# Where the opening of a fused kernel's second part puts its elementwise work

## The chip, the cores and the metric

The program runs on one core of a Trainium2 chip. Its time is the device time in microseconds (us) of one launch, which computes the whole output. The figure for a kernel is the median of its runs.

## What is computed

Two networks run one after the other on 512 tokens of width 1024, in float32. The first has two layers of differential attention beside a gated recurrence, each with an MLP and a gated embedding. Its last step is a norm, `rms_norm(h, g_final)`, and the result is the input of the second network. That is a state-space mixer (8 groups of heads, 6 chunks of 128 tokens, two directions) over 256 context tokens and the 512 tokens, then an attention mixer. Each mixer's input is normed, scaled and shifted:

```python
x = rms_norm(h, g_final)                                   # end of the first network
in_lat = rmsnorm(h_lat, norm_w[i]) * (1.0 + scl) + sh      # h_lat = x for i = 0
in_ctx = rmsnorm(h_ctx, norm_w[i]) * (1.0 + sclc) + shc
z, xbc, dt = split(in @ in_w)                              # state-space mixer
xbc = silu(conv5(xbc) + b); dt = softplus(dt + bias)       # steps: 64 columns
la = cumsum(dt * a) per chunk; to_end = exp(la_end - la) * dt
h_lat = h_lat + gt * out(...)
```

So at the seam there are two norms in a row, and x itself is kept as the residual of the first mixer.

## The kernel before

Activations lie with features on the 128 partitions (8 blocks, `KB`) and tokens along the free dimension. A float32 product is made of three products of rounded parts: each operand is split into a rounded `hi` and the rest `lo` (`value - hi`). Weights stream from memory as 1 MB tiles in two slots. SyncE issues the loads. GpSimd splits each tile when TensorE has released its slot: four roundings (L404), then four rests (L408), in one long loop over pairs of tiles (`split_pair`). TensorE's `dense` (its products are L797) goes through the 8 feature blocks of a tile and can wait before each block.

Every engine runs its own instruction list in order and waits on semaphores. These lists are written out by hand, so the order of the work around the change is the order in the source.

*The seam.* TensorE sums squares over the features and gives two rows, broadcast over the partitions: PSUM bank 6 holds the reciprocal root of the first norm, bank 7 the factor of the second norm on top of the first. VectorE then works on a feature block b of 512 tokens with three instructions: `scaled` (L2296) multiplies the residual `hres` by g_final and bank 6, in place; `normed_in` (L2303) multiplies it by bank 7 into `tin`; `rest_in` (L2307) writes `inlo`. Between the last two ScalarE scales and shifts `tin` (L1590) and rounds it to `inhi` (L1591). `tin` has two buffers, so `normed_in(b)` waits for `rest_in(b-2)`. VectorE also makes both rests of the context (L2292). ScalarE then issues the DMA that spills `hres` to memory (L1592); it is read back, and its place reused, in the groups.

*The steps.* TensorE's first product is that of the step tile, fed block by block (`in_lo`). VectorE adds the bias (L2333), TensorE turns it token-major (L818), VectorE copies it (L2336), ScalarE takes Abs and Exp (L1624, L1626), VectorE runs the softplus (L2885 to L2893), and L2339, L2340 add the positive part. Meanwhile TensorE computes four blocks of 128 channels (`T_XS0`, `T_BC0`), and later their cumulative sums (L831, L833).

*The first filters.* For each of the four blocks ScalarE copies it from PSUM and makes the first tap (`first_copy`, L1611 to L1613, L1598), VectorE adds four taps (`first_conv`, L2363), ScalarE takes a tanh (`conv_tanh`, L1617, L1618) and VectorE gates (`silu`, L2377). Between blocks 1 and 2 VectorE reads the cumulative sums (L2396 to L2400), and ScalarE makes exponentials of them (L1641 to L1644). After block 3 VectorE makes two tables (L2408, L2409) and clears five tiles (L2410 to L2415). The last of the clears but one releases ScalarE into the first group.

*The first group.* ScalarE: a tanh (L1659), a copy (L1664), copies of the turned chunks (L1668, L1669). TensorE turns chunks (L862 to L864), four before it needs ScalarE's first copies.

*The half-norms.* After the groups the residual is normed again in two halves of 384 tokens (`half_in`): VectorE's product (L2445), ScalarE's scale and shift by segment of tokens (L1761) and rounding (L1765), VectorE's rest (L2439). The first half has two segments, since context and tokens have different factors, the second one.

*Small parts.* `second_params` (L1935 to L1952) prepares scale and shift vectors during the first network's last stage. `busy` (L479) gives TensorE small products while it waits.

## Time and profile before

| | us |
|---|---|
| runs shown | 2400.40, 2401.42, 2402.52 (median 2401.42) |
| the profiled execution: its time | 2399.92 |
| its span, first to last instruction | 2397.9 |
| mean granted clock of TensorE | 0.990 |
| busy: TensorE, VectorE | 2310.2 (96%), 1497.4 (62%) |
| busy: ScalarE, GpSimd | 755.2 (31%), 1418.5 (59%) |
| chain that ended last | TensorE 75%, VectorE 16%, "issue" 3%, ScalarE 3%, DMA 1%, GpSimd 1% |

In the profile PE is TensorE, PEld its weight loads, DVE VectorE, ACT ScalarE, POOL GpSimd. Times run from the span's first instruction. A line such as L797 is a line of the kernel's source. "Idle before <-" names what ended the idle time of the engine ahead of an instruction. An instruction's length takes in any time in which it stands started but held up. The chain is followed back from the last instruction, at each step to what released it. Clock 1.00 stands for 2.4 GHz, 0.5 for 1.2 GHz. The second part begins near 1266 us, its groups at 1336 us, its attention near 2048 us.

### The profile page before, as it was taken

The page shows a single profiled execution, that of the slowest core. Times are in us where ns is not written, and L with a number is a line of the kernel's source. Part 1 is how long each engine was busy: PE and PEld are TensorE (multiplying, and loading weights), DVE is VectorE, ACT ScalarE, POOL GpSimd, SP SyncE. Part 2 cuts the span into 40 slices and gives each one's busy share as a digit, 9 for nine tenths or more (in the row PEclk, how much of TensorE's full clock was granted, in tenths as well). Part 3 has the DMA queues.
Part 4 walks back from the last instruction along what each step waited for, and adds up shares of the span by engine and source line. Part 5 has one row for each costly group of instructions (what it writes and reads, how often), then busy time and mean ns, then how long its engine had stood idle before and what let it go on. Part 6 is the DMA issues. An engine that isn't in the chain of part 4 may idle for free.

```text
span 2397.9 us, 32255 instructions
## 1 busy us (share of the span) xinstructions
PE 2310.2 (96%) x11638; PEld 1905.7 (79%) x11638; DVE 1497.4 (62%) x1868; ACT 755.2 (31%) x1579; POOL 1418.5 (59%) x1248
## 2 busy tenths in 40 slices
PE   8999999999999899999998999999999998999998
PEld 6767888888777688888877899999999987776446
DVE  7964333444784552434478888788788787518653
ACT  2453200112333430110135434334334334533551
POOL 8735767777776277777784353453453451256785
PEclk9999999999999999999999999999999998999999
DMA  4321334433224033434332110111110112021212
GB/s 166 112 74 71 132 140 141 158 132 121 90 74 129 30 129 121 152 134 155 106 116 102 53 53 35 52 52 35 52 52 35 52 53 82 29 95 58 52 28 71
DMA packets 41596, 211.31 MB, mean 88 GB/s; under 512 B 5408, under 2 KB 9504, under 8 KB 21536
## 3 DMA queue, kind: packets, MB, share of 16 engines
q1 hardware_dynamic: 27456, 164.84, 19.4%
q10 hardware_dynamic: 14048, 45.17, 5.6%
q8 instruction: 67, 1.10, 0.2%
q14 instruction: 25, 0.20, 0.0%
HBM read 197.67 MB, written 7.34 MB: 85 GB/s over the span
## 4 chain that ended last, share of the span: by engine, by line
PE 75%; DVE 16%; issue 3%; ACT 3%; DMA 1%; POOL 1%; ACTq 0%; DVEq 0%; SPq 0%; POOLq 0%
PE ps L505 39%; PE ps L797 15%; PE ps L1044 5%; DVE convd L2363 2%; PE ps L1161 2%; PE ps L894 1%; PE ps L1143 1%; DVE wdec L2507 1%; PE ps L917 1%; PE ps L599 1%; PE ps L641 1%; PE ps L1148 1%; DVE convd L2377 1%; PE ps L622 1%; DVE convd L2359 1%
## 5 line engine op out<-in xcount | busy, mean ns | idle before, releaser
L404 POOL TENSOR_SCALAR whi<-wraw 128x512 fp32r<-128x512 f32 x564 | 385.4, 712 | 909.5 <-PE ps L797 423.0
L408 POOL TENSOR_TENSOR wlo<-wraw,whi 128x512 fp32r<-128x512 f32 x568 | 859.4, 1544 | 0.8 <-ACT whi L1401 0.8
L505 PE MATMUL ps<-uhi,whi 128*128 128x512 f32 x896 | 353.4, 394 | 15.5 <-POOL wlo L390 11.0
L505 PE MATMUL ps<-uhi,wlo 128*128 128x512 f32 x896 | 349.5, 390 | 0.0
L505 PE MATMUL ps<-ulo,whi 128*128 128x512 f32 x896 | 349.5, 390 | 0.0
L797 PE MATMUL ps<-inhi,whi 128*128 128x384 f32 (+1 forms) x784 | 243.1, 345 | 5.5 <-DVE inlo L2307 4.3
L797 PE MATMUL ps<-inhi,wlo 128*128 128x384 f32 (+1 forms) x784 | 235.9, 335 | 0.0
L797 PE MATMUL ps<-inlo,whi 128*128 128x384 f32 (+1 forms) x784 | 235.8, 335 | 0.0
L505 PEld LDWEIGHTS ps<-uhi,whi 128*128 128x128 f32 x896 | 168.7, 188 | 54.3 <-POOL wlo L390 11.0
L2182 DVE TENSOR_TENSOR h<-h,ps 128x1024 f32<-128x1024 f32 x40 | 48.8, 1221 | 241.4 <-PE ps L505 241.4
L505 PE MATMUL ps<-hidhi,whi 128*128 128x512 f32 x512 | 199.2, 389 | 0.0
L505 PE MATMUL ps<-hidhi,wlo 128*128 128x512 f32 x512 | 199.2, 389 | 0.0
L505 PE MATMUL ps<-hidlo,whi 128*128 128x512 f32 x512 | 199.2, 389 | 0.0
L505 PEld LDWEIGHTS ps<-uhi,wlo 128*128 128x128 f32 x896 | 168.8, 188 | 36.3 <-issue 1.4
L505 PEld LDWEIGHTS ps<-ulo,whi 128*128 128x128 f32 x896 | 168.7, 188 | 35.4
L1492 ACT ACTIVATE hsq<-hm 128x1024 f32<-128x1024 f32 x32 | 34.0, 1064 | 488.2 <-DVE hm L2213 488.2
L797 PEld LDWEIGHTS ps<-inhi,whi 128*128 128x128 f32 (+1 forms) x784 | 143.7, 187 | 16.8 <-issue 8.6
L2363 DVE SCALAR_TENSOR_TENSOR convd<-raw,cpg,convd 128x770 f32<-128x770 f32 x128 | 149.0, 1164 | 5.0 <-ACT convd L1598 2.6
L2213 DVE SCALAR_TENSOR_TENSOR hm<-ps,rstd 128x1024 f32<-128x1024 f32 x32 | 39.2, 1225 | 173.3 <-PE ps L505 173.2
L797 PEld LDWEIGHTS ps<-inhi,wlo 128*128 128x128 f32 (+1 forms) x784 | 144.5, 187 | 1.0
L797 PEld LDWEIGHTS ps<-inlo,whi 128*128 128x128 f32 (+1 forms) x784 | 144.4, 187 | 0.8
L1690 ACT ACTIVATE ebuf<-ps,tabg 128x128 f32<-128x128 f32 x384 | 104.4, 387 | 116.8 <-PE ps L906 83.8
(450 smaller groups left out, 4628.1 us busy)
## 6 DMA issues: line engine op xcount, KB each, us to landing
wraw<-in_wstream SPq DMA_DIRECT2D x150, 1024.0 KB, 4.8
modraw<-in_modw ACTq DMA_DIRECT2D x48, 512.0 KB, 3.3
hspill<-hres ACTq DMA_DIRECT2D x1, 3072.0 KB, 10.6
...
```

Source lines behind the costliest of these rows:

```text
L404: pool.tensor_scalar(whi[:, s, c], wraw[:, s, c], 1.0, 0.0, ALU.mult, ALU.add).then_inc(wraw_read, 1)
L408: ins = pool.tensor_tensor(wlo[:, s, c], wraw[:, s, c], whi[:, s, c].bitcast(F32), ALU.subtract)
L505: mm = pe.matmul(ps[:, 2 * bank + m, :], a[:, w, c:c + P], b[:, kb, :], start=(n == 0 and i == 0), stop=(n == KB - 1 and i == 2))
L599: pe.matmul(ps[:, SCORE_BANKS(n)[c], 0:w], q, proj[64 * c:64 * c + 64, K0 + hd, 0:w], start=True, stop=False)
L797: mm = pe.matmul(ps[0:width, q + half, 0:HALF], a[:, s, c:c + width], b[:, kb, half * HALF:(half + 1) * HALF], start=(n == 0), stop=(n == ...
L1044: mm = pe.matmul(ps[:, q + m, :], a[:, k % 2, c:c + P], b[:, kb, t0:t0 + S], start=(kb == 0 and i == 0), stop=(kb == KB - 1 and i == 2))
L1161: mm = pe.matmul(ps[64 * e:64 * e + 64, 2, :], vtok2[:, kb, HD * j:HD * j + HD], pT2[(NC * b + kb) % RING][:, e, :], start=(kb == 0), stop ...
L1492: A(hsq[n % 2][:, :, :], hm[n % 2][:, :, :], ACT.Square).then_inc(L["sqh_r"], 1)
L1690: ins = A(ebuf[:, d, r, :], ps[:, 4 + d, r * P:(r + 1) * P], ACT.Exp, bias=tabg[:, K_NB + 2 * c + d, r:r + 1])
L2182: V.tensor_tensor(h[:, 2 * j:2 * j + 2, :], h[:, 2 * j:2 * j + 2, :], TWO(bank), ALU.add).then_inc(L["h_r"], 1)
L2213: V.scalar_tensor_tensor(out=hm[n % 2][:, :, :], in0=TWO(n % 2), scalar=0.0, in1=rstd2, op0=ALU.max, op1=ALU.mult).then_inc(L["m_r"], 1)
L2363: ins = V.scalar_tensor_tensor(out=o, in0=r[:, n:n + CW], scalar=cpg[:, 6 * b + n:6 * b + n + 1], in1=o, op0=ALU.mult, op1=ALU.add)
```

## The change

- The factor of `normed_in` now holds g_final, the second norm's weight and 1 + scale at once (`modA` is multiplied by g_final), and bank 7 holds the reciprocal root of both norms together. VectorE's `scaled` is gone. The shift is added by ScalarE in its rounding pass and by VectorE in its rest, both as one instruction a block. The same is done in the half-norms, where product and rest now go by segment.
- The residual is scaled by GpSimd, in place, two instructions a block, each block after VectorE's product has read it; ScalarE copies bank 6 into `row6` for that. GpSimd also makes the second half of the context rest. Its long loop is cut in three, and these instructions stand between the split of tile 103 and that of tile 104.
- ScalarE reads the step product, TensorE turns it inside the next tile (ahead of its third block), Abs reads PSUM. The spill is issued behind GpSimd's last block and ahead of Abs.
- VectorE no longer copies the cumulative sums: ScalarE copies one into the table and takes its exponentials from PSUM. The order of filters and gates changes on VectorE and ScalarE, and the two tables come ahead of the last filter.
- Three clears go to a place ahead of the norm terms on VectorE, two to GpSimd behind the split of tile 106. The first group waits for the tables and not for a clear. Counts of semaphores that stand later are adapted.

```diff
--- before.py
+++ after.py
@@ gpsimd @@
+        def first_zeros():
+            pool.wait_ge(dt_d, DT_END)
+            pool.memset(lablk[:, :, :].bitcast(F32), 0.0)
+            pool.wait_ge(spill, 16)
+            pool.memset(sqz[:, :, :], 0.0).then_inc(sqz_r, 1)
...
-        with pool.Fori(NFM // 2 + 1, (T_ATT + 11) // 2) as i:
+        with pool.Fori(NFM // 2 + 1, T_XS0 // 2 + 1) as i:
+            split_pair(i)
+        pool.wait_ge(ctx_hi, 2)
+        pool.tensor_tensor(inlo[:, 4:8, 0:CTX], ctxn[:, 4:8, :], inhi[:, 4:8, 0:CTX].bitcast(F32), ALU.subtract
+                           ).then_inc(ctx_t, 1)
+        pool.wait_ge(rr_r, 1)
+        for b in range(KB):
+            pool.wait_ge(in_t, b + 1)
+            pool.tensor_scalar(hres[:, b, CTX:T], hres[:, b, CTX:T], p2[:, C2_GF + b:C2_GF + b + 1], None, ALU.mult
+                               ).then_inc(n_x, 1)
+            pool.wait_ge(n_x, 2 * b + 1)
+            pool.tensor_tensor(hres[:, b, CTX:T], hres[:, b, CTX:T], row6[:, :], ALU.mult).then_inc(n_x, 1)
+        split_pair(T_G0 // 2)
+        split_pair(T_G0 // 2 + 1, between=first_zeros)
+        with pool.Fori(T_G0 // 2 + 2, (T_ATT + 11) // 2) as i:
@@ tensor @@
         def turn_dt():
-            pe.wait_ge(dt_d, 1)
+            pe.wait_ge(dt_a, 2)
...
-        turn_dt()
         wait_split(T_XS0)
-        dense(T_XS0 % 2, lambda i: i * TM, P, IN, EIGHT, False, 2, None)
+        dense(T_XS0 % 2, lambda i: i * TM, P, IN, EIGHT, False, 2, None, lambda kb: turn_dt() if kb == 2 else None)
@@ scalar @@
+        act.wait_ge(rb_ps, 2)
+        A(row6[:, :], ps[:, 6, :], ACT.Copy).then_inc(rr_r, 1)
         for b in range(KB):
             act.wait_ge(in_t, b + 1)
-            st(A(tin[:, b % 2, 0:S], tin[:, b % 2, 0:S], ACT.Identity, scale=modA[:, b, 0:1], bias=modv[0][:, b, 0:1]))
-            A(inhi[:, b, CTX:T], tin[:, b % 2, 0:S], ACT.Copy).then_inc(in_hi, 1)
-        act.dma_start(hspill, hres[:, :, :]).then_inc(spill, 16)
+            A(inhi[:, b, CTX:T], tin[:, b % 2, 0:S], ACT.Identity, bias=modv[0][:, b, 0:1]).then_inc(in_hi, 1)
...
-        act.wait_ge(dt_d, 2)
-        A(dtw[1][:, :, :], dtw[0][:, :, :], ACT.Abs).then_inc(dt_a, 1)
-        act.wait_ge(dt_a, 2)
+        done_wait(T_DT)
+        A(halves(dtT[:, :]), ps[0:64, 0:2, 0:HALF], ACT.Identity, bias=p2[0:64, C2_DTB:C2_DTB + 1]).then_inc(dt_a, 1)
+        act.wait_ge(n_x, 2 * KB)
+        act.dma_start(hspill, hres[:, :, :]).then_inc(spill, 16)
+        act.wait_ge(dt_p, 1)
+        A(dtw[1][:, :, :].rearrange("p c r -> p (c r)"), ps[:, 4, 0:384], ACT.Abs).then_inc(dt_a, 1)
+        act.wait_ge(dt_a, 3)
...
         first_copy(0, 1, None)
+        conv_tanh(0, 0)
         first_copy(1, None, T_XS0)
-        conv_tanh(0, 0)
         conv_tanh(0, 1)
         first_copy(2, 2, None)
-        act.wait_ge(dt_d, DT_C)
+        act.wait_ge(dt_p, 2)
+        A(flat(K_G), ps[:, 5, 0:384], ACT.Copy).then_inc(dt_a, 1)
+        act.wait_ge(dt_d, DT_C)
         A(w(6), w(6), ACT.Ln).then_inc(dt_a, 1)
-        A(flat(K_EXLA), w(3), ACT.Exp)
-        A(flat(K_DEC), w(4), ACT.Exp)
+        A(flat(K_EXLA), ps[:, 5, 0:384], ACT.Exp)
+        A(flat(K_DEC), ps[:, 6, 0:384], ACT.Exp)
...
-        act.wait_ge(acc_r2, 1)
+        act.wait_ge(dt_d, DT_END)
...
(half_in, for each segment)
-                    ins = A(tin[:, b % 2, t0:t1], tin[:, b % 2, t0:t1], ACT.Identity, scale=modA[:, b, c:c + 1],
-                            bias=modv[1][:, b, c:c + 1])
-                st(ins)
-                A(inhi[:, b, hs], tin[:, b % 2, hs], ACT.Copy).then_inc(in_hi, 1)
+                    ins = A(inhi[:, b, t0:t1], tin[:, b % 2, t0:t1], ACT.Identity, bias=modv[1][:, b, c:c + 1])
+                ins.then_inc(in_hi, 1)
@@ vector @@
+            st(V.tensor_tensor(modA[:, :, 0], modA[:, :, 0], gf, ALU.mult))
...
+        V.memset(larow[:, :, :].bitcast(F32), 0.0)
+        V.tensor_copy(lapick[:, :], picks[:, :])
+        V.memset(acc[:, :], 0.0).then_inc(acc_r2, 1)
         dve.wait_ge(L["mod_T"], DEPTH * PER["mod_T"] + 1)
...
-        st(V.reciprocal(dcol[:, 16:24], dcol[:, 8:16]))
-        V.tensor_tensor(dcol[:, 20:24], dcol[:, 20:24], dcol[:, 8:12], ALU.mult).then_inc(n_rs, 1)
+        V.reciprocal(dcol[:, 16:24], dcol[:, 8:16]).then_inc(n_rs, 1)
...
(scaled(b) is removed; normed_in and rest_in of block b:)
-            V.tensor_tensor(tin[:, b % 2, 0:S], hres[:, b, CTX:T], ps[:, 7, :], ALU.mult).then_inc(in_t, 1)
+            V.scalar_tensor_tensor(out=tin[:, b % 2, 0:S], in0=hres[:, b, CTX:T], scalar=modA[:, b, 0:1], in1=ps[:, 7, :],
+                                   op0=ALU.mult, op1=ALU.mult).then_inc(in_t, 1)
...
-            V.tensor_tensor(inlo[:, b, CTX:T], tin[:, b % 2, 0:S], inhi[:, b, CTX:T].bitcast(F32), ALU.subtract
+            V.scalar_tensor_tensor(out=inlo[:, b, CTX:T], in0=tin[:, b % 2, 0:S], scalar=modv[0][:, b, 0:1],
+                                   in1=inhi[:, b, CTX:T].bitcast(F32), op0=ALU.add, op1=ALU.subtract).then_inc(in_lo, 1)
...
         first_conv(0)
+        silu(0, 0)
         first_conv(1)
-        silu(0, 0)
         silu(0, 1)
-        dt(V.tensor_copy(w(3), ps[:, 5, 0:384]))
-        dt(V.tensor_copy(tab[:, K_G:K_G + 2 * NC, :].rearrange("p c r -> p (c r)"), ps[:, 5, 0:384]))
-        dt(V.tensor_copy(w(4), ps[:, 6, 0:384]))
-        dt(V.tensor_tensor(w(5), w(4), w(3), ALU.subtract))
         dt(V.tensor_scalar(w(6), w(2), 1e-37, None, ALU.max))
+        dve.wait_ge(dt_a, 5)
+        dt(V.tensor_tensor(w(5), ps[:, 6, 0:384], flat(K_G), ALU.subtract))
         first_conv(2)
+        dve.wait_ge(dt_a, 7)
+        dt(V.tensor_tensor(flat(K_NB), w(6), flat(K_G), ALU.subtract))
+        dt(V.tensor_tensor(flat(K_TE), w(5), w(2), ALU.mult))
         first_conv(3)
         silu(0, 2)
         silu(0, 3)
...
```

## Rows read from the trace of the kernel before

**Rows 1.** Busy time of each engine by window, 1272 to 1287 us: length, busy us (instructions), clock, DMA

```profile
1272.00:1287.00 15.00, 11.15 (x48) 6.73 (x48) 12.89 (x26) 11.08 (x16) 0.00 (x0) 0.89 0.13 52
```

**Rows 2.** Timeline of VectorE: start, length, line, operation, output<-inputs, idle before

```profile
1265.74 0.16 DVE L2282 TENSOR_SCALAR dcol<-ps 128x4 f32<-128x4 f32 x1 [3.65 <-PE ps L735]
...
1276.50 0.68 DVE L2307 TENSOR_TENSOR inlo<-tin,inhi 128x512 fp32r<-128x512 f32 x1
1277.11 0.74 DVE L2296 SCALAR_TENSOR_TENSOR hres<-hres,p,ps 128x512 f32<-128x512 f32 x1
...
1278.36 0.68 DVE L2307 TENSOR_TENSOR inlo<-tin,inhi 128x512 fp32r<-128x512 f32 x1
...
1285.10 0.69 DVE L2307 TENSOR_TENSOR inlo<-tin,inhi 128x512 fp32r<-128x512 f32 x1 [0.70 <-ACT inhi L1591]
```

**Rows 3.** Timeline of GpSimd near the kernel's start

```profile
26.12 0.62 POOL L388 TENSOR_SCALAR whi<-wraw 128x512 fp32r<-128x512 f32 x1
26.82 1.28 POOL L390 TENSOR_TENSOR wlo<-wraw,whi 128x512 fp32r<-128x512 f32 x1
```

**Rows 4.** Instructions of one line: ns min/median/max, first and last start

```profile
L408 POOL TENSOR_TENSOR wlo<-wraw,whi x3: 1261/1700/1715, 1259.8 to 1263.2; 128x512 fp32r<-128x512 f32 x3
...
L408 POOL TENSOR_TENSOR wlo<-wraw,whi x4: 1983/2007/2011, 1310.5 to 1316.4; 128x512 fp32r<-128x512 f32 x4
...
L2377 DVE SCALAR_TENSOR_TENSOR convd<-raw,convd x32: 949/962/2046, 1313.2 to 1966.2; 128x770 f32<-128x770 f32 x32
```

**Rows 5.** Timeline of VectorE in the first half-norm

```profile
2050.77 1.65 DVE L2439 TENSOR_TENSOR inlo<-tin,inhi 128x384 fp32r<-128x384 f32 x1 [1.14 <-ACT inhi L1765]
2052.46 0.56 DVE L2445 TENSOR_TENSOR tin<-oacc,ps 128x384 f32<-128x384 f32 x1
```

**Rows 6.** Timeline of all engines at the hand-over to softplus

```profile
1287.15 1.01 DVE L2333 TENSOR_SCALAR dtT<-ps,p 64x768 f32<-64x768 f32 x1 [1.30 <-PE ps L797]
...
1288.22 0.59 PE L818 MATMUL ps<-ident,dtT 64*128 64x64 f32 x6 [1.10 <-DVE dtT L2333]
...
1290.70 0.45 DVE L2885 TENSOR_SCALAR dtw<-dtw 128x384 f32<-128x384 f32 x1 [1.22 <-ACT dtw L1626]
```

**Rows 7.** Timeline of VectorE through the first filters

```profile
1307.74 5.56 DVE L2363 SCALAR_TENSOR_TENSOR convd<-raw,cpg,convd 128x770 f32<-128x770 f32 x4 [0.96 <-ACT convd L1598]
...
1317.16 0.55 DVE L2396 COPY dtw<-ps 128x384 f32<-128x384 f32 x1
...
1319.52 0.36 DVE L2400 TENSOR_SCALAR dtw<-dtw 128x384 f32<-128x384 f32 x1
...
1325.69 7.35 DVE L2363 SCALAR_TENSOR_TENSOR convd<-raw,cpg,convd 128x770 f32<-128x770 f32 x4 [1.59 <-ACT convd L1598]
```

**Rows 8.** Timeline of ScalarE through the first filters

```profile
1313.67 0.61 ACT L1618 ACTIVATE raw<-convd 128x512 f32<-128x512 f32 x1
1315.36 0.39 ACT L1611 ACTIVATE raw<-ps 128x256 f32<-128x256 f32 x1 [1.09 <-DVE convd L2377]
...
1316.34 1.03 ACT L1598 ACTIVATE convd<-raw,cpg 128x770 f32<-128x770 f32 x1
```

**Rows 9.** Timelines of TensorE and of ScalarE at the first group's start

```profile
1336.21 0.41 PE L862 MATMUL ps<-ident,convd 128*128 128x128 f32 x2 [2.90 <-DVE convd L2377]
...
1341.03 0.45 PE L862 MATMUL ps<-ident,convd 128*128 128x128 f32 x2 [0.77 <-ACT btok L1669]
...
1338.79 0.81 ACT L1659 ACTIVATE zs<-ps 128x768 f32<-128x768 f32 x1 [4.78 <-DVE acc L2413]
```

**Rows 10.** Timeline of ScalarE in the first and the second half-norm

```profile
2057.74 0.99 ACT L1761 ACTIVATE tin<-tin,modv,modA 128x256 f32<-128x256 f32 x2
2058.76 0.52 ACT L1765 ACTIVATE inhi<-tin 128x384 fp32r<-128x384 f32 x1
...
2077.77 0.71 ACT L1761 ACTIVATE tin<-tin,modv,modA 128x384 f32<-128x384 f32 x1
```

**Rows 11.** Chain of waits in order of time: start, us, engine, line

```profile
1233.04 0.19 DVE modA L1936
```

More of the change, by code:

```diff
@@ L181, in build @@
     ctxr = at("ctxr", 138, [P, CTX])
+    row6 = at("row6", 186.375, [P, S])
     dcol = at("dcol", 142, [P, 32])
@@ L394, in _, with split_pair @@
             pool.sem_inc(wfree, 1)
-        def split_pair(i, rounded=None):
+        def first_zeros():
[3 more added lines that the diff above has]
+            pool.memset(sqz[:, :, :], 0.0).then_inc(sqz_r, 1)
+        def split_pair(i, rounded=None, between=None):
             for s in range(2):
+                if s and between:
+                    between()
                 pool.wait_ge(wland[s], i * 16 + 16)
@@ L767, in half_sums @@
                 busy(2, 7)
-            pe.wait_ge(rr_r, 2 + h)
+            pe.wait_ge(rr_r, 3 + h)
             for c in range(3):
@@ L812, in _, with input_wait @@
         busy(11, 0)
-        dense(T_DT % 2, lambda i: i * 64, 64, IN, EIGHT, True, 0, None, lambda kb: pe.wait_ge(in_lo, kb + 1))
+        def input_wait(kb):
+            pe.wait_ge(in_lo, kb + 1)
+            if kb == 4:
+                pe.wait_ge(ctx_t, 2)
+        dense(T_DT % 2, lambda i: i * 64, 64, IN, EIGHT, True, 0, None, input_wait)
         def turn_dt():
-            pe.wait_ge(dt_d, 1)
+            pe.wait_ge(dt_a, 2)
             for c in range(NC):
@@ L984, in _ @@
         group(GROUPS - 1, True)
-        pe.wait_ge(rr_r, 1)
+        pe.wait_ge(rr_r, 2)
         half_sums(0)
@@ L1671, in group @@
             act.wait_ge(lr_ps, g + 1)
+            act.wait_ge(sqz_r, g + 1)
             for r in range(HPG):
@@ L1744, in half_squares @@
                 n = KB * hf + j
-                act.wait_ge(n_x, KB + n + 1)
+                act.wait_ge(n_x, 2 * KB + n + 1)
                 if n >= 6:
@@ L2331, in _ @@
         dt = Chain(dve, dt_d)
-        done_wait(T_DT)
-        dt(V.tensor_scalar(halves(dtT[:, :]), ps[0:64, 0:2, 0:HALF], p2[0:64, C2_DTB:C2_DTB + 1], None, ALU.add))
         w = lambda n: dtw[n][:, :, :].rearrange("p c r -> p (c r)")
-        dve.wait_ge(dt_p, 1)
-        dt(V.tensor_copy(w(0), ps[:, 4, 0:384]))
-        dve.wait_ge(dt_a, 3)
+        dve.wait_ge(dt_a, 4)
         softplus(V, dt, w(2), w(1), w(3), w(4), w(5))
-        dt(V.tensor_scalar(w(0), w(0), 0.0, None, ALU.max))
-        dt(V.tensor_tensor(w(2), w(2), w(0), ALU.add))
+        dt(V.scalar_tensor_tensor(out=w(2), in0=ps[:, 4, 0:384], scalar=0.0, in1=w(2), op0=ALU.max, op1=ALU.add))
         dt(V.scalar_tensor_tensor(out=tab[:, K_G:K_G + 2 * NC, :].rearrange("p (c d) r -> p c (d r)", d=2),
@@ L2438, in lo @@
                 dve.wait_ge(in_hi, base + b + 1)
-                V.tensor_tensor(inlo[:, b, hs], tin[:, b % 2, hs], inhi[:, b, hs].bitcast(F32), ALU.subtract
-                                ).then_inc(in_lo, 1)
+                for t0, t1, c in HALF_SEG[hf]:
+                    ins = V.scalar_tensor_tensor(out=inlo[:, b, t0:t1], in0=tin[:, b % 2, t0:t1], scalar=modv[1][:, b, c:c + 1],
+                                                 in1=inhi[:, b, t0:t1].bitcast(F32), op0=ALU.add, op1=ALU.subtract)
+                ins.then_inc(in_lo, 1)
             dve.wait_ge(rb_ps, 4 + hf)
@@ L2444, in half_in @@
                     dve.wait_ge(in_lo, base + b - 1)
-                V.tensor_tensor(tin[:, b % 2, hs], oacc[:, b, hs], ps[:, 4 + hf, 0:HALF], ALU.mult).then_inc(in_t, 1)
+                for t0, t1, c in HALF_SEG[hf]:
+                    ins = V.scalar_tensor_tensor(out=tin[:, b % 2, t0:t1], in0=oacc[:, b, t0:t1], scalar=modA[:, b, c:c + 1],
+                                                 in1=ps[:, 4 + hf, t0 - hf * HALF:t1 - hf * HALF], op0=ALU.mult, op1=ALU.mult)
+                ins.then_inc(in_t, 1)
                 if b:
@@ L2613, in group @@
                 dve.wait_ge(spill, 32)
-                dve.wait_ge(rr_r, 1)
+                dve.wait_ge(rr_r, 2)
                 for j in range(KB):
@@ L2868 @@
 CST = 16 * 2
-DT_G, DT_C = 18, 23
+DT_G, DT_C, DT_END = 15, 17, 19
 GROUP_STEPS = 52
```

37 lines of the change are left out of this document (7 added, 30 removed).

## The prediction

> **What bounds the kernel now.** I read the page's chain of waits first: three quarters of it are TensorE's, so only stretches in which it leaves TensorE can give much. This change touches two of them, the opening of the second part (1266 to 1342 us) and the two half-norms before its attention (2048 to 2087). Next I read busy times by window. From 1272 to 1287 VectorE is busy 12.89 of 15 us, TensorE 11.15 at a mean clock of 0.89, GpSimd not at all [rows 1]: TensorE is fed one feature block at a time by VectorE. VectorE's timeline gives the pitch, three instructions a block, from 1276.50 to 1278.36, so 1.86 us; the last rest ends at 1285.79 [rows 2]. Then the timeline of all engines shows a hand-over: step sums read at 1287.15, turned at 1288.22, softplus from 1290.70 [rows 6]. From there VectorE's softplus and filters set the end, up to the group's turns at 1336.21 [rows 7, 9].
>
> **The port.** GpSimd, idle there, now gets eight scale-and-multiply pairs, so the price hangs on what the two engines do to each other. A GpSimd TENSOR_SCALAR and the TENSOR_TENSOR that depends on it, 128x512, take 0.62, a gap of 0.08, and 1.28 [rows 3]: 1.96 a pair with the overlap at the join. Beside VectorE instructions with two SBUF inputs the same TENSOR_TENSOR has a median of 1.70 (VectorE's 512 wide) and 2.01 (770 wide) [rows 4]. VectorE suffers likewise: the 384-wide rest, with two SBUF inputs, takes 1.65 while GpSimd splits, but the product that reads PSUM stays at 0.56 [rows 5]. The Trainium skill, "SBUF — State Buffer", section Who interferes with whom, says that a VectorE instruction with two SBUF inputs and a GpSimd instruction that reads SBUF exclude each other for a whole instruction, and that one with a single SBUF input is free. It speaks against this change, and the trace agrees in kind. Taken strictly, a cycle below would be an estimated 0.62 + 0.08 + 1.28 + 0.69 = 2.67, and the step product would end 1.6 us later than I say. I go by the rows, in which part of the two overlaps.
>
> **Part 1, the norm loop.** VectorE keeps the product (from PSUM, now with a factor, so 0.74 as the scaling took) and the rest (0.69) [rows 2]; the separate scaling leaves. Alone that is 0.74 + 0.69, less 0.08 overlap, plus 0.03 for the wait: 1.38 a block. With GpSimd: its scaling and gap (0.70) fall beside the product, then its TENSOR_TENSOR and VectorE's rest meet, about 1.66 for the two (1.70 less the join). Cycle 2.36, longer than the 1.86 it replaces. GpSimd starts late, behind its half of the context rest (two 512 widths, 2.5, from about 1267.4). So the first rests are cheap: product 0 near 1268.8, rest 0 done at 1271.1, rest 1 at 1272.8; five at 2.36 give 1284.6, and the last, against a short scaling, 1285.6. Before: 1285.79. Gain 0.2, of which one removed 0.16 us instruction ahead of the row sums is most. ScalarE's single pass a block lies between a plain copy and the scale-and-shift pass (0.52 and 0.71 at 384 wide [rows 10]); at this pitch it is hidden, and so is its copy of the row for GpSimd. GpSimd then has two blocks left and ends near 1285.0 + 1.70 + 1.96 = 1288.7. Its next split moves to 1288.7 to 1295.8; TensorE wants it at about 1304: nothing. The 3 MB spill is issued behind GpSimd's last block, 48 us ahead of its first reader: nothing.
>
> **Part 2, the hand-over.** The step product ends at 1286.9. ScalarE reads the sums (VectorE took 1.01) beside two weight blocks of TensorE (2.1), then the turns 0.59, Abs and Exp 1.2 [rows 6]: softplus near 1290.8 against 1290.70. Nothing. TensorE itself runs 1.5 earlier, only to wait later. The clears go into VectorE's idle 3.65 us ahead of the norm terms [rows 2]: nothing. One small instruction (0.19) joins a stretch on the chain at 1233 [rows 11]: +0.2, which cancels the gain of part 1.
>
> **Part 3, softplus.** One clamp of 0.36 less, but GpSimd's later split meets one more two-input instruction (+0.9): it ends 0.5 later.
>
> **Part 4, the filters.** Before, 1302.3 to 1335.9. Terms:
> - Five small instructions, 1317.16 to 1319.88, 2.7 [rows 7], become two, 1.0: -1.7.
> - The two table products now stand before the last filter, under a split: 2 x 0.6 and 1.2 for collisions: +2.4.
> - The order filter, gate, filter, gate makes VectorE wait for ScalarE's tanh twice. Filter 1 ended at 1313.30, its tanh at 1314.28 [rows 7, 8]; with the wait's latency 1.07 each: +2.1. VectorE's waits of 0.96 and 1.59 for ScalarE's first taps [rows 7] go: -2.5.
> - The second small instruction waits for ScalarE, which must first copy block 2 (1315.36 to 1317.37 [rows 8]) and then the sums (0.5), against 1.3 of gate (0.96 [rows 4]) and clamp: +1.1.
> - The last tanh is no longer covered: +0.3; joins: -0.3.
> Sum +1.4; with part 3 the last gate ends 1.9 later, near 1337.8. TensorE has idled 3.4 then, not 2.9 [rows 9].
>
> **Part 5, the group's start.** ScalarE's first tanh waited 4.78 behind VectorE's clears, TensorE 0.77 for ScalarE's copies [rows 9]. Both go. ScalarE gains some 3.4 on the gates, but TensorE spends 4 us on turns before it needs a copy, so the path gains only 0.8. GpSimd's clears come behind its third split, near 1335, their first reader about ten us later: nothing. Sum +1.1.
>
> **Part 6, the half-norms.** First half: ScalarE paced it, 0.99 + 0.52 [rows 10], 1.43 to 1.57 a block. VectorE now has four instructions (widths 256 and 128, twice), 1.48 a block, and both rests of a block meet GpSimd's four: +0.9. Second half: 0.71 + 0.52, 1.24 a block, becomes 1.21 with no wait for ScalarE between, and TensorE's last block starts 1.0 earlier. Together -0.1.
>
> **The sum** is +1.0. The profiled execution took 2399.92 (span 2397.9 and 2.0 around it), 1.50 below the median shown, 2401.42. So 2400.9 for such a one, and 2402.4 for the median.
>
> **Unknown costs.** GpSimd's scaling by a per-partition factor has no row. Below: the 0.62 of [rows 3]; above: 1.28, as for two inputs. I take 0.62, the same operation and shape. GpSimd ends at 1288.7 and the turns are ready at 1289.6, so only over 0.12 a block it holds up the spill and with it Abs. The bias-only pass: no effect at either end.
>
> **Rivals.**
> - *The multiplies do not collide* (VectorE may reach the port first; my order rests on 0.2 us). Blocks at 1.38 end the step product near 1282.0, GpSimd at 1269.9 + 8 x 1.96 = 1285.6, softplus 4 us earlier: 2402.4 - 4.3 = 2398.1. Against it: [rows 4, 5]. Chance 0.14.
> - *The new waits do not show.* Filters go on under tanh and sums as before (-3.2), and TensorE turns at full clock after its idle time (-2.0): 2397.2. For it: GpSimd's splits shift against the filters. Against: the waits are written into the order. Chance 0.14.
> - *Slower: ScalarE stands behind GpSimd.* The spill's wait for all sixteen results stands ahead of Abs. Past 0.12 us a block every further 0.1 is 0.8 on softplus, and the next split falls on its two-input instructions. At 0.6: GpSimd ends at 1293.4, softplus 3.7 later, 1.3 of collisions: 2407.4. Chance 0.16.
> The forecast keeps 0.56, its own range 2400 to 2405. About 0.2%, 4.8 us, is what a measurement of this kernel can tell from no change. Faster by more (below 2396.6): half of the second rival, 0.07, some of the first, 0.04, and 0.02 for both together: 0.13. Slower by more (above 2406.2): most of the third, 0.11, and 0.01 besides: 0.12. The range 2396.8 to 2407.4 reaches to all three and leaves their tails out.
>
> **What would show it.** In the norm loop: VectorE rests of 1.6 us, GpSimd's multiplies at 1.3, pitch 2.3 to 2.4, last rest near 1285.6; softplus near 1290.8; waits of VectorE of about 1.1 before gates 0 and 1 and before the second small instruction; the last gate near 1337.8; ScalarE's first tanh of the group just before it. A pitch near 1.4, softplus at 1287, or gates without waits would prove me wrong downwards; GpSimd pairs over 2.1 standing alone, upwards.

## The result, and the profile after

The changed kernel takes 2408.66 us (median of 7, 2407.16 to 2409.35), the kernel before 2402.52 in the same comparison: ratio 1.0025, 95% interval 1.0015 to 1.0035. That is 6.1 us slower, where 1.0 was forecast, and above the range. The profiled execution took 2408.38, span 2406.6, 8.7 over that of before.

Stage by stage, in us, worked out from starts and ends in the timelines. "Norm terms" begin where VectorE's row of 1265.74 in [rows 2] does. The reciprocal is softplus' second instruction (L2886 before), the step table its last (L2342), and the decay turn is what TensorE does behind the first group's turned chunks (L880). The columns behind the second belong to experiments below.

| stage | before | after | e1 | e3 | e9 | e6 | e7 |
|---|---|---|---|---|---|---|---|
| norm terms to last rest | 20.05 | 18.45 | 18.40 | 19.20 | 21.22 | 18.03 | 18.02 |
| last rest to softplus' reciprocal | 5.39 | 13.58 | 5.97 | 6.63 | 7.08 | 5.43 | 5.43 |
| from there to the step table | 11.15 | 16.44 | 15.95 | 9.87 | 10.75 | 10.74 | 10.75 |
| filters, to the last gate | 33.53 | 31.65 | 34.25 | 35.25 | 35.24 | 35.23 | 32.97 |
| last gate to the group's decay turn | 10.51 | 9.50 | 7.88 | 8.01 | 7.86 | 8.02 | 9.53 |
| sum | 80.63 | 89.62 | 82.45 | 78.96 | 82.15 | 77.45 | 76.70 |

The opening is 9.0 longer. Ahead of it the changed kernel's trace is 1.9 earlier, behind it 1.7 later, which makes the 8.7. The opening's two losses, 8.2 ahead of softplus' reciprocal and 5.3 behind it, are larger than the whole; the filters, the norm loop and the group's start give 4.5 back.

GpSimd's timeline of the changed kernel (start, length, line, operation, output<-inputs, idle before), and under it ScalarE's, as in [rows 3, 6]:

```profile
1266.22 2.52 POOL L430 TENSOR_TENSOR inlo<-ctxn,inhi 128x1024 fp32r<-128x1024 f32 x1 [1.29 <-ACT inhi L1616]
1268.72 1.57 POOL L435 TENSOR_SCALAR hres<-hres,p 128x512 f32<-128x512 f32 x1
1270.37 1.28 POOL L438 TENSOR_TENSOR hres<-hres,row 128x512 f32<-128x512 f32 x1
...
1274.99 2.01 POOL L435 TENSOR_SCALAR hres<-hres,p 128x512 f32<-128x512 f32 x1
1277.08 1.30 POOL L438 TENSOR_TENSOR hres<-hres,row 128x512 f32<-128x512 f32 x1
1278.35 2.01 POOL L435 TENSOR_SCALAR hres<-hres,p 128x512 f32<-128x512 f32 x1
...
1292.55 1.29 POOL L438 TENSOR_TENSOR hres<-hres,row 128x512 f32<-128x512 f32 x1
1293.81 2.49 POOL L414 TENSOR_SCALAR whi<-wraw 128x512 fp32r<-128x512 f32 x4
```

```profile
1283.64 0.90 ACT L1654 ACTIVATE dtT<-ps,p 64x768 f32<-64x768 f32 x1 [1.60 <-PE ps L824]
1293.87 0.34 ACTq L1656 DMA_DIRECT2D hspill<-hres  x1
1294.26 0.49 ACT L1658 ACTIVATE dtw<-ps 128x384 f32<-128x384 f32 x1 [9.72 <-POOL hres L438]
```

The scaling takes 1.57 alone and 2.01 beside VectorE, not the 0.62 of [rows 3]. GpSimd ends at 1293.84 instead of the forecast 1288.7, and ScalarE, whose step sums were read by 1284.54, idles 9.72 for it ahead of Abs. The splits of two tiles follow only from 1293.81 on, so they now lie on softplus. VectorE's timeline shows both, and what the prediction says of the loop and of the filters (beside [rows 2, 6, 7]):

```profile
1274.35 1.22 DVE L2337 SCALAR_TENSOR_TENSOR inlo<-tin,modv,inhi 128x512 fp32r<-128x512 f32 x1
1275.60 0.75 DVE L2332 SCALAR_TENSOR_TENSOR tin<-hres,modA,ps 128x512 f32<-128x512 f32 x1
1276.27 0.75 DVE L2337 SCALAR_TENSOR_TENSOR inlo<-tin,modv,inhi 128x512 fp32r<-128x512 f32 x1
1277.05 0.75 DVE L2332 SCALAR_TENSOR_TENSOR tin<-hres,modA,ps 128x512 f32<-128x512 f32 x1
1277.71 1.22 DVE L2337 SCALAR_TENSOR_TENSOR inlo<-tin,modv,inhi 128x512 fp32r<-128x512 f32 x1
...
1295.34 0.48 DVE L2902 TENSOR_SCALAR dtw<-dtw 128x384 f32<-128x384 f32 x1 [13.01 <-ACT dtw L1660]
...
1299.26 1.54 DVE L2905 TENSOR_TENSOR dtw<-dtw 128x384 f32<-128x384 f32 x1
1300.83 1.31 DVE L2906 TENSOR_SCALAR dtw<-dtw 128x384 f32<-128x384 f32 x1
...
1302.17 5.67 DVE L2908 SCALAR_TENSOR_TENSOR dtw<-dtw,dtw 128x384 f32<-128x384 f32 x6
...
1317.75 0.96 DVE L2396 SCALAR_TENSOR_TENSOR convd<-raw,convd 128x770 f32<-128x770 f32 x1 [1.00 <-ACT raw L1648]
1319.64 4.19 DVE L2382 SCALAR_TENSOR_TENSOR convd<-raw,cpg,convd 128x770 f32<-128x770 f32 x4 [0.92 <-ACT convd L1628]
1324.84 0.96 DVE L2396 SCALAR_TENSOR_TENSOR convd<-raw,convd 128x770 f32<-128x770 f32 x1 [1.01 <-ACT raw L1648]
...
1327.17 0.56 DVE L2417 TENSOR_TENSOR dtw<-ps,tab 128x384 f32<-128x384 f32 x1 [1.10 <-ACT tab L1676]
```

The reader is to see four things. Rests take 1.22 and 0.75 by turns, so two blocks take 3.36: the loop's pitch is 1.68, not 2.36. Softplus waits 13.01. Its instructions then take up to 1.54 where the same shape takes 0.56 without a split beside it. The waits of 1.00, 1.01 and 1.10 in the filters are those forecast; the one of 0.92 for ScalarE's first tap is one that the prediction had struck out. The filters are 1.9 shorter, where 1.4 longer was forecast, because a split has moved ahead onto softplus. Before, it lay on the second filter (5.56 for four taps in [rows 7], 4.19 here) and on the first two gates (0.96 each here), as VectorE's timeline of the kernel before shows:

```profile
1313.23 4.01 DVE L2377 SCALAR_TENSOR_TENSOR convd<-raw,convd 128x770 f32<-128x770 f32 x2
```

Windows from 1272 to 1287 as in [rows 1] (length, then busy us of TensorE, its weight loads, VectorE, ScalarE and GpSimd, then clock and DMA): GpSimd busy 14.58 of 15, VectorE 10.03.

```profile
1272.00:1287.00 15.00, 12.20 (x65) 8.51 (x66) 10.03 (x18) 6.07 (x8) 14.58 (x10) 1.00 0.00 1
```

### The profile page after: what moved, and what is told of

It reads as the page before. It is cut to its first block, busy times and chain, and to the rows that moved or that the text cites. A ratio compares the mean times of both kernels' runs of the same rounds, so it can differ in the third digit from the quotient of the medians.

```text
span 2406.6 us, 32231 instructions
## 1 busy us (share of the span) xinstructions
PE 2310.5 (96%) x11638; PEld 1907.6 (79%) x11638; DVE 1493.6 (62%) x1867; ACT 742.2 (31%) x1558; POOL 1447.7 (60%) x1267
## 4 chain that ended last, share of the span: by engine, by line
PE 75%; DVE 16%; issue 3%; ACT 2%; POOL 2%; DMA 1%; ACTq 0%; DVEq 0%; SPq 0%; POOLq 0%
PE ps L532 39%; PE ps L824 14%; PE ps L1074 5%; DVE convd L2382 3%; PE ps L1191 2%; PE ps L924 1%; PE ps L1173 1%; DVE wdec L2524 1%; PE ps L626 1%; PE ps L668 1%; PE ps L947 1%; PE ps L1178 1%; PE ps L649 1%; DVE convd L2396 1%; DVE convd L2378 1%
```

## The experiments

Theory T: one mis-sized instruction on GpSimd, a wait that makes ScalarE stand behind it, and splits pushed onto softplus are the whole loss. The experiments bear out the first two; the splits turn out to cost less than they seem to. The rivals have letters in the expectations. Ratios are to the kernel before, with 95% intervals.

### e1: the wait moved

```diff
         done_wait(T_DT)
         A(halves(dtT[:, :]), ...)
-        act.wait_ge(n_x, 2 * KB)
-        act.dma_start(hspill, hres[:, :, :]).then_inc(spill, 16)
         act.wait_ge(dt_p, 1)
         A(dtw[1]..., ps[:, 4, 0:384], ACT.Abs)
         A(dtw[1]..., ACT.Exp, scale=-1.0)
+        act.wait_ge(n_x, 2 * KB)
+        act.dma_start(hspill, hres[:, :, :]).then_inc(spill, 16)
```

> The changed kernel with one thing moved: ScalarE's wait for GpSimd's sixteen results, and the spill that it guards, stand behind Exp instead of ahead of Abs. Theory T (GpSimd's scaling by a per-partition factor takes 1.57 us instead of 0.62, GpSimd ends at 1293.8, and ScalarE's Abs waits behind it): GpSimd's scaling stays at 1.6 to 2.0 us and its last block still ends near 1293.8, but Abs starts when the turns are done, near 1287.5, softplus near 1289 instead of 1295.3. Softplus then lies beside the last three GpSimd pairs and the split of tile 104 from 1293.9 on, so it gets back some of its length: tab ends between 1303 and 1307 instead of 1312.3; whole time 2400 to 2404, against 2408.7. Rival R1 (the wait costs little by itself; the later splits falling on softplus and the filters are what costs, wherever softplus starts): tab ends at 1309 or later, whole time 2406 to 2408. Rival R2 (the order of the filters or the tail is what costs): 2408, with the tab earlier and the last gate not.

Measured: 2402.74, ratio 1.0003 (0.9994 to 1.0012). ScalarE's and GpSimd's timelines:

```profile
1290.40 0.49 ACT L1656 ACTIVATE dtw<-ps 128x384 f32<-128x384 f32 x1 [1.71 <-PE ps L850]
```

```profile
1295.17 1.87 POOL L435 TENSOR_SCALAR hres<-hres,p 128x512 f32<-128x512 f32 x1
1297.13 1.29 POOL L438 TENSOR_TENSOR hres<-hres,row 128x512 f32<-128x512 f32 x1
```

Abs waits for the turns alone. GpSimd is as slow as ever and ends at 1298.41. This execution ran 4.2 later than the changed kernel's from its norm terms on, so stages are to be compared, not times of day: the stage of the hand-over falls from 13.58 to 5.97, softplus stays long (15.95), since the splits are still late. The opening is 7.2 shorter than the changed kernel's, and the ratio falls by 0.0022, which is 5.3. So the wait by itself carries nearly all of the loss: R1 falls, and R2 with it. (1.6 of the 7.2 is at the group's start, of which more below.)

### e2 and e8: which property makes the scaling slow

e2 changes one operand, `p2[...]` to `1.0`, and so leaves out the multiplication by g_final:

```diff
-            pool.tensor_scalar(hres[:, b, CTX:T], hres[:, b, CTX:T], p2[:, C2_GF + b:C2_GF + b + 1], None, ALU.mult
+            pool.tensor_scalar(hres[:, b, CTX:T], hres[:, b, CTX:T], 1.0, None, ALU.mult
```

> The changed kernel with GpSimd's scaling by the constant 1.0 instead of the per-partition factor g_final (it leaves out the multiplication of the residual by g_final; everything else is as it was). Theory T (the per-partition factor is what makes the scaling slow): scaling 0.62 us alone and at most 0.9 beside VectorE, the pair 1.96 alone, GpSimd's last block ends near 1287, Abs no longer waits for it, softplus starts near 1288.5, tab ends near 1302, the whole time is 2399 to 2403. Rival R4 (the slow scaling comes from the place or the data, in-place in the residual or beside TensorE's and VectorE's traffic, and not from the form): the scaling stays at 1.5 us or more, nothing else moves, and the time stays near 2408. Rival R2 (the order of the filters is what costs): scaling 0.62, softplus early, but the whole time above 2405.

Measured: 2406.64, ratio 1.0014 (1.0005 to 1.0023). The constant takes 1.49 alone and 1.93 beside VectorE:

```profile
1282.71 1.93 POOL L435 TENSOR_SCALAR hres<-hres 128x512 f32<-128x512 f32 x1
...
1285.98 1.49 POOL L435 TENSOR_SCALAR hres<-hres 128x512 f32<-128x512 f32 x1
```

So theory T as first put was wrong in its cause: the per-partition factor costs 0.07. R4 had the length and the time nearly right, but in-place use, which it offered as one reason, falls in e8. What else differs from the split's rounding of [rows 3]? It is written with two operations (times 1.0, plus 0.0), its output is rounded, and it isn't in place. e8 gives each block a form of its own (so it leaves out parts of the scaling):

```diff
+            f0, f1, o0, src = [(gf, None, x, x), (1.0, None, x, x), (1.0, 0.0, x, x), (gf, 0.0, x, x),
+                               (1.0, 0.0, x.bitcast(F32R), x), (gf, None, x.bitcast(F32R), x),
+                               (1.0, None, x, row6[:, :]), (gf, 0.0, x.bitcast(F32R), x)][b]
```

> The changed kernel with eight different forms of GpSimd's scaling, one a block (it leaves out parts of the residual's scaling, and rounds some of it). Blocks 0 to 7: 0 as in the change (factor g_final, one operation); 1 the constant 1.0, one operation; 2 the constants 1.0 and 0.0, multiply then add, as the splits have it; 3 g_final and 0.0, multiply then add; 4 as 2 with the output rounded to fp32r; 5 as 0 with the output rounded; 6 the constant 1.0, one operation, read from the row and not in place; 7 as 3 with the output rounded. Theory T1 (an absent second operation is what makes it slow): 2, 3, 4 and 7 take 0.62 to 0.95, the others 1.5 to 2.0. Theory T2 (the fp32r output makes the splits fast): only 4, 5 and 7 are fast. Theory T3 (reading and writing the same place is what makes it slow): only 6 is fast. Theory T4 (only all constants with two operations are fast): 2 and 4 fast, 3 and 7 slow.

GpSimd's timeline, scalings of blocks 0 to 7 (L441 is written with one operation, L443 with two), and the first rounding of the next split:

```profile
1271.33 1.56 POOL L441 TENSOR_SCALAR hres<-hres,p 128x512 f32<-128x512 f32 x1
...
1274.23 1.93 POOL L441 TENSOR_SCALAR hres<-hres 128x512 f32<-128x512 f32 x1
...
1277.49 1.06 POOL L443 TENSOR_SCALAR hres<-hres 128x512 f32<-128x512 f32 x1
...
1279.90 1.13 POOL L443 TENSOR_SCALAR hres<-hres,p 128x512 f32<-128x512 f32 x1
...
1282.37 1.06 POOL L443 TENSOR_SCALAR hres<-hres 128x512 fp32r<-128x512 f32 x1
...
1284.77 1.99 POOL L441 TENSOR_SCALAR hres<-hres,p 128x512 fp32r<-128x512 f32 x1
...
1288.10 1.49 POOL L441 TENSOR_SCALAR hres<-row 128x512 f32<-128x512 f32 x1
...
1290.94 0.69 POOL L443 TENSOR_SCALAR hres<-hres,p 128x512 fp32r<-128x512 f32 x1
...
1292.97 0.62 POOL L414 TENSOR_SCALAR whi<-wraw 128x512 fp32r<-128x512 f32 x1
```

T1 holds in all eight, only that the two-operation forms beside VectorE are up to 0.18 above the 0.95 that it allowed; T2, T3 and T4 fall. With two operations the row shows 0.62 (the split's) to 0.69 alone and 1.06 to 1.13 beside VectorE; with one, 1.49 to 1.56 and 1.93 to 1.99. Its one execution took 2405.63. Rounding and place change nothing. Leaving the second operation out makes GpSimd's instruction 0.87 us longer.

### e9 and e10: the kernel that was priced

```diff
-            pool.tensor_scalar(hres[:, b, CTX:T], hres[:, b, CTX:T], p2[:, C2_GF + b:C2_GF + b + 1], None, ALU.mult
-                               ).then_inc(n_x, 1)
+            pool.tensor_scalar(hres[:, b, CTX:T], hres[:, b, CTX:T], p2[:, C2_GF + b:C2_GF + b + 1], 0.0, ALU.mult,
+                               ALU.add).then_inc(n_x, 1)
```

> The changed kernel with GpSimd's scaling written as two operations, times g_final and plus 0.0; the result is the same. Theory T (the one-operation form of the scaling is the whole loss; this kernel is the one that the prediction priced): scaling 0.69 alone and 1.13 beside VectorE, pair 2.06 alone, blocks of about 2.5 in the loop, GpSimd's last block ends near 1287.5 to 1288.5, Abs starts within 1 us of it, softplus near 1290, tab near 1301 to 1303, whole time 2399 to 2403. Rival R1 (the spill's wait ahead of Abs costs several us even so): tab at 1305 or later, whole time 2404 or more. Rival R2 (something else of the change costs the rest): whole time 2406 or more.

Measured: 2401.61, ratio 0.9996 (0.9987 to 1.0004): the whole loss is gone with one more operation, and R1 and R2 fall. GpSimd's timeline, then VectorE's of the same stretch, then ScalarE's Abs:

```profile
1277.18 1.28 POOL L438 TENSOR_TENSOR hres<-hres,row 128x512 f32<-128x512 f32 x1
1278.44 1.13 POOL L435 TENSOR_SCALAR hres<-hres,p 128x512 f32<-128x512 f32 x1
1279.65 1.27 POOL L438 TENSOR_TENSOR hres<-hres,row 128x512 f32<-128x512 f32 x1
...
1286.95 1.29 POOL L438 TENSOR_TENSOR hres<-hres,row 128x512 f32<-128x512 f32 x1
```

```profile
1276.58 0.75 DVE L2332 SCALAR_TENSOR_TENSOR tin<-hres,modA,ps 128x512 f32<-128x512 f32 x1
1277.24 1.77 DVE L2337 SCALAR_TENSOR_TENSOR inlo<-tin,modv,inhi 128x512 fp32r<-128x512 f32 x1
1279.05 0.75 DVE L2332 SCALAR_TENSOR_TENSOR tin<-hres,modA,ps 128x512 f32<-128x512 f32 x1
```

```profile
1290.67 0.49 ACT L1658 ACTIVATE dtw<-ps 128x384 f32<-128x384 f32 x1 [1.73 <-PE ps L850]
```

The pitch is 2.47 and GpSimd ends at 1288.23. Abs waits for the turns, not for GpSimd, and starts 2.4 behind it, not within 1 as T had it. Against e9, the changed kernel's opening is 7.5 longer: the hand-over 6.5, softplus 5.7 and the group's start 1.6 longer, the filters 3.6 and the norm loop 2.8 shorter. So the late splits cost 2.1 net, since most of what they take on softplus they no longer take on the filters.

e1 and e9 mend the same loss in two ways. In e1 GpSimd is as slow as ever, and its opening is 82.45 against 82.15, its ratio 1.0003 against 0.9996 with intervals that overlap. The slow scaling costs little or nothing unless something critical waits for it. e10 adds e1's move to e9.

> As e9_two_operations, with ScalarE's wait for GpSimd and the spill behind Exp as well. Theory T: only the 0.5 to 1 us by which GpSimd still ends behind the turns is to be had, so softplus starts 0.5 to 1.5 us before that of e9, and the time is within 1.5 us below it. Rival R1: 3 us or more faster than e9.

Measured: 2401.75, ratio 0.9994 (0.9985 to 1.0003). Nothing more, as T has it; R1 falls. Its stages are 21.26, 5.79, 11.71, 34.90 and 9.51, in sum 83.16. The hand-over is 1.3 shorter than in e9, but not for T's reason: in e9 too Abs did not wait for GpSimd. It is TensorE's clock, as below.

### e3 and e6: the scaling elsewhere

e3 gives it back to VectorE, without the copy of the row:

```diff
-(GpSimd's two instructions a block, ScalarE's copy of bank 6)
         for b in range(KB):
             normed_in(b)
             if b:
                 rest_in(b - 1)
+                scaled(b - 1)
...
(scaled as in the kernel before, the last block behind the loop; counts of semaphores adapted)
```

> The changed kernel with the residual's scaling back on VectorE (one scalar_tensor_tensor a block, g_final and the row from PSUM, behind the rest of the block before), and GpSimd's eight pairs and the copy of the row gone. Theory T: all that the change lost comes from the pairs on GpSimd. VectorE's cycle is 0.74 + 0.69 + 0.6, about 2.0 us a block, last rest near 1285; softplus near 1290, splits where they were before the change, tab near 1302.5; the filters cost what the prediction has in part 4, so the whole time is 2400 to 2404. Rival R2 (order of the filters and their waits): the tab back at 1302.5 but the last gate still 5 us or more late, whole time above 2405. Rival R3 (the half-norms or the tail): above 2405 with the last gate near 1338.

Measured: 2398.31, ratio 0.9983 (0.9974 to 0.9992), 1.7 below what T gave. Three instructions of 0.74 start 0.66 apart, a pitch of 1.98. Softplus takes 9.87 from its reciprocal on, since the split ends (1292.6) while the reciprocal runs. Its R2 and R3 fall.

e6 leaves GpSimd only the row, and has e1's move of the spill as well:

```diff
             A(inhi[:, b, CTX:T], tin[:, b % 2, 0:S], ACT.Identity, bias=modv[0][:, b, 0:1]).then_inc(in_hi, 1)
+            A(hres[:, b, CTX:T], hres[:, b, CTX:T], ACT.Copy, scale=p2[:, C2_GF + b:C2_GF + b + 1]).then_inc(Ls["p_r"], 1)
...
-            pool.tensor_scalar(...)
             pool.tensor_tensor(hres[:, b, CTX:T], hres[:, b, CTX:T], row6[:, :], ALU.mult).then_inc(n_x, 1)
...
(ScalarE's wait for GpSimd and the spill stand behind Exp, as in e1)
```

> The changed kernel with the scaling by g_final on ScalarE (one more pass a block, 0.72 us), GpSimd left with the multiplication by the row, and the spill behind Exp. Theory T (GpSimd's slow scaling is the whole loss): GpSimd takes 1.3 us a block, less than VectorE's cycle of 1.4 to 1.7, its last block ends within 2 us of the last rest, near 1283; Abs and softplus start near 1286.5, splits come 4 us or more earlier than before the change; tab near 1298 to 1300, whole time 2394 to 2399, so at least as fast as with the scaling on VectorE. Rival R5 (GpSimd's multiplies stretch VectorE's rests to 1.6 as the prediction said, so nothing is won over the scaling on VectorE): last rest near 1285.6, whole time 2399 to 2403.

Measured: 2397.60, ratio 0.9982 (0.9973 to 0.9992). GpSimd's timeline groups six multiplies, 1.70 apart; VectorE's rests take 1.00:

```profile
1272.33 10.23 POOL L435 TENSOR_TENSOR hres<-hres,row 128x512 f32<-128x512 f32 x6
```

```profile
1277.02 1.00 DVE L2335 SCALAR_TENSOR_TENSOR inlo<-tin,modv,inhi 128x512 fp32r<-128x512 f32 x1
...
1286.45 0.36 DVE L2900 TENSOR_SCALAR dtw<-dtw 128x384 f32<-128x384 f32 x1 [4.97 <-ACT dtw L1656]
```

The ratios put e3 4.1 and e6 4.3 below the kernel before, and so some 10 below the changed one; their intervals don't tell one from the other.

### e4, e5, e7: the other parts

e4 is the kernel before with the new order of filters and gates alone.

```diff
         first_conv(0)
+        silu(0, 0)
         first_conv(1)
-        silu(0, 0)
...
         first_copy(0, 1, None)
+        conv_tanh(0, 0)
         first_copy(1, None, T_XS0)
-        conv_tanh(0, 0)
```

> The kernel before with only the order of the first group changed: filter, gate, filter, gate on VectorE, and ScalarE's first tanh ahead of its second copy. Theory T (the order costs next to nothing): VectorE waits about 1.0 us for tanh ahead of gate 0 and gate 1, and no longer 0.96 and 1.59 for ScalarE's first taps; the last gate of the opening within 1 us of the kernel before, the whole time within 2 us of it. Rival R2 (the order is what costs): the last gate 3 us or more later and the whole time 2405 or more.

Measured: 2401.76, ratio 0.9997 (0.9988 to 1.0006). The last gate is 0.5 later by the clock of the trace and 0.8 counted from the norm terms, with waits of 1.01 ahead of both gates. Of the two waits for ScalarE's first taps (0.96 and 1.59) that the order was to remove, 0.92 and 0.69 are still there. What comes behind is another matter, in TensorE's and ScalarE's timelines (beside [rows 9]):

```profile
1341.54 0.44 PE L862 MATMUL ps<-ident,convd 128*128 128x128 f32 x2 [2.43 <-ACT btok L1669]
```

```profile
1339.31 0.81 ACT L1659 ACTIVATE zs<-ps 128x768 f32<-128x768 f32 x1 [5.89 <-DVE acc L2413]
```

With the old clears, ScalarE is held 5.89 and TensorE 2.43 (0.77 before), so the start of the group loses 1.6. The runs don't show the 2.4 that the two make: the median is below that of before, and the interval ends 1.4 above.

e7 is e6 with the old order:

```diff
         first_conv(0)
-        silu(0, 0)
         first_conv(1)
+        silu(0, 0)
...
         first_copy(0, 1, None)
-        conv_tanh(0, 0)
         first_copy(1, None, T_XS0)
+        conv_tanh(0, 0)
```

> As e6_scalar_scales, with the old order of the opening's filters: filter, filter, gate, gate on VectorE, and ScalarE's first tanh behind its second copy. If the prediction's part 4 is right (the new order costs two waits of 1.07 and saves 2.5), the last gate is within 0.5 us of e6's and the time within 1.5 us. Rival R2 (the new order costs): 2 us or more faster than e6. Rival R6 (the new order pays at the group's start, where ScalarE's tanh comes ahead of its copies): 1 us or more slower than e6.

Measured: 2398.02, ratio 0.9976 (0.9967 to 0.9985). Equal to e6 within the intervals, but not stage by stage: its filters are 2.3 shorter, where the expectation allowed 0.5, and its group's start 1.5 longer. VectorE's timeline shows why: with the old order filter 1 follows filter 0 without a wait for its first tap, and filter 3 waits 0.64, so there was hardly anything left for the new order to save.

```profile
1300.03 10.25 DVE L2380 SCALAR_TENSOR_TENSOR convd<-raw,cpg,convd 128x770 f32<-128x770 f32 x8 [0.26 <-DVE tab L2359]
...
1322.38 6.46 DVE L2380 SCALAR_TENSOR_TENSOR convd<-raw,cpg,convd 128x770 f32<-128x770 f32 x4 [0.64 <-ACT convd L1626]
```

e5 has the half-norms alone, on the kernel before:

```diff
-                    ins = A(tin[:, b % 2, t0:t1], tin[:, b % 2, t0:t1], ACT.Identity, scale=modA[...], bias=modv[1][...])
-                A(inhi[:, b, hs], tin[:, b % 2, hs], ACT.Copy).then_inc(in_hi, 1)
+                    ins = A(inhi[:, b, t0:t1], tin[:, b % 2, t0:t1], ACT.Identity, bias=modv[1][:, b, c:c + 1])
...
(VectorE: product and rest by segment, as in the change)
```

> The kernel before with only the half-norms of the change. Theory T: the first half loses about 1.0 and the second gains about 1.0, so the time is that of the kernel before within 1 us, 2402 to 2404. Rival R3 (the half-norms or what follows them add to the loss, since the changed kernel's trace loses another 1.5 us behind them): 2404.5 or more.

Measured: 2401.32, ratio 1.0000 (0.9990 to 1.0009). R3 falls.

### b2: the kernel before, once more

> The kernel before, once more. Theory V (the 1.9 us that the changed kernel's trace gains ahead of the change, and the 1.4 that it loses behind the half-norms, are differences from one execution to the next): from its norm terms (1265.74 in the first trace) to other stages this execution agrees with the first within 0.3 us inside the opening, and stands off it by 1 to 3 us at the stretches ahead of 1266 or behind 2225. Rival: both stretches take the same time as in the first trace within 0.3 us, and the changed kernel really differs there.

Its profiled execution took 2401.57. Every stage up to the second half-norm agrees with the first trace within 0.2, and the attention behind is 1.55 longer, as the changed kernel's is by 1.54. It is so, within 0.1, in every kernel of the table and in e4 and e5. So that 1.5 is no effect of the change; the first profile of before was short there. Ahead of the opening it agrees within 0.15, so it does not show the 1.9. Over the other kernels that stretch spreads from 2.4 earlier (e6) to 2.3 later (e1), with the same work in it; e6 and e7, identical there, differ by 2.2.

## Why the prediction was wrong

**The step that failed** stands under "Unknown costs": "below: the 0.62 of [rows 3]; above: 1.28, as for two inputs. I take 0.62, the same operation and shape." It measured 1.57, above even the upper bound (1.49 with a constant factor), and e8 shows why the nearest row misled: the same operation and shape, but written with two operations. The bound "as for two inputs" rested on the idea that one input can't cost more than two; it can. The third rival had the mechanism that came (the spill's wait ahead of Abs, then splits on softplus). At its 0.6 a block it gave softplus 3.7 later; at the real 0.95, counted from the norm terms, GpSimd ended 7.1 later than forecast and softplus started 6.6 later than before. Its 1.3 for collisions is of the size of the net 2.1 against e9: softplus grew by 5.3, and the filters came out 3.3 below their forecast.

**The norm loop** was priced at a pitch of 2.36 with rests of 1.6. The changed kernel shows 1.68. The slow GpSimd meets the rest only every second block, so VectorE was faster for it. e9, with GpSimd at the price assumed, shows 2.47 and rests of 1.77, and e6 1.70 for multiply and rest, where the working had 1.66. The collision price was right; that the two engines fall into step depends on their lengths.

The weighing of the rule was not right. In e9 a rest that starts 0.06 behind a multiply ends 0.55 behind the multiply's end (1279.01 against 1278.46), and the scaling queued under it takes 1.13, which is 0.44 of waiting and its own 0.69. So the cycle is 1.28, 0.55 and 0.69 less the joins: they take turns, whole. The Trainium skill, "SBUF — State Buffer", section Who interferes with whom, says just that of two SBUF inputs against a reading GpSimd; the trace agrees with it for this pair more closely than with the partial overlap I took. The estimate by it, 2.67, was 0.2 too long: it put in the rest's full 0.69, while the rows show 0.44 to 0.55 in which one engine holds up the other. For the scaling with one operation the trace does not agree: a rest that starts under it keeps its 0.75 (last section), and the measurement decides.

The prediction also put that section of the Trainium skill too shortly where it says that a single SBUF input is free; the section excepts VectorE's 2-port modes. Here softplus' TENSOR_SCALAR, with one SBUF input, takes 0.36 [rows 7] and 1.31 beside a split (1300.83 above), so it is not free, and part 3 had no price for it.

**The hand-over** would have been late a little even at the priced length: 7.08 in e9 against 5.39. That is TensorE: from 1284 to 1288.1 the granted clock is 0.54, so mostly at the lower level, 1.2 GHz, after a stretch in which it idled 1.2 a block. In e10, with the same loop, the clock falls earlier in it, where VectorE sets the pace (mean 0.89 from 1270 to 1285, as in [rows 1]); it is 1.00 at the hand-over, and the stage takes 5.79. The prediction had no term for it.

```profile
1284.00:1288.10 4.10, 4.09 (x14) 3.03 (x15) 1.11 (x7) 0.63 (x3) 3.93 (x4) 0.54 0.02 4
```

**The filters** came out right in their sum, and by luck. Forecast +1.4 with splits where they were; e3, e6 and e9 show +1.7. But in part 4's terms the new order comes to about -0.1, and e4 shows +0.8 and e6 against e7 +2.3. The term at fault is the 2.5 for ScalarE's first taps: a wait of 0.92 stays ahead of filter 1, and without the new order e7 has only 0.64 of such waits. The other terms come to +1.5 in the forecast and to -0.6 in e7, and the two errors cancel.

**The group's start** was forecast to gain 0.8 and gained 1.0 in the changed kernel. In e9, e6 and e3 it gains 2.5 to 2.7. The difference is the clock again. TensorE's windows of 5 us from its first turn, changed kernel, e9, e3 and e10:

```profile
1344.20:1349.20 5.00, 4.90 (x30) 4.93 (x31) 3.63 (x9) 3.60 (x11) 0.06 (x1) 0.66 0.46 188
```

```profile
1338.40:1343.40 5.00, 4.92 (x40) 4.96 (x41) 4.59 (x10) 4.28 (x15) 0.00 (x0) 1.00 0.26 110
```

```profile
1335.70:1340.70 5.00, 4.85 (x39) 4.88 (x40) 4.71 (x11) 4.13 (x14) 0.00 (x0) 1.00 0.25 105
```

```profile
1339.00:1344.00 5.00, 4.99 (x31) 5.00 (x31) 3.95 (x9) 3.90 (x12) 0.00 (x0) 0.66 0.06 20
```

TensorE idled 3.24 us ahead of the first, 0.76 ahead of the second, 1.88 ahead of the third and 1.92 ahead of the fourth. In the kernel before it idled 2.90 [rows 9] and had 0.66, in e7 3.14 and 0.66, in e6 0.70 and 1.00. The idle time just ahead does not settle it: e3 and e10 are alike in it and differ in the clock. What goes with it is the clock of the ten us before: 0.80 to 0.88 in all seven kernels whose turns had 1.00 (e1, e2, e3, e4, e6, e8, e9), 0.94 in e10, and 1.00 in before, e5, e7 and the changed kernel, whose turns had 0.66. In the seven the stretch at the lower level fell on TensorE's products beside the last filters, where VectorE sets the pace. The second rival's saving from turns at full clock thus came true in them, and is 1.5 to 1.6; no run shows what decides where the clock falls, so it counts as luck.

**The half-norms**: forecast -0.1. From VectorE's first product in them to ScalarE's first read behind them it is 38.57 before, 38.29 in e5 and 38.30 in the changed kernel: -0.3, after a first half that ends 0.7 later, where 0.9 was forecast.

**The sum** for the kernel that was priced was +1.0; e9's median is 1.6 below before's and its ratio 1.0 below, with the interval from 3.1 below to 1.0 above. Part of that is luck. Up to the last gate e9 is 4.2 later than before, where +1.9 was forecast, and the group's start gives 2.65 back, where 0.8 was. What stays open: why the ratio of every kernel with an opening other than before's is better than its opening says, by 1.1 (e1, e6) to 3.9 us (e10), in e9 2.5 and in the changed kernel 3.0; the 1.9 ahead of the opening, which spreads by kernel and execution without a cause that I can name; and why the median of the changed kernel is only 6.1 above where its trace has 7.2 without the 1.5 of the attention.
